# Attention scores of two heads side by side, and the latent's norm two rounds sooner

## What is computed

```python
# layer 0, mixer_a: indexer over 16 heads of 64, 128 of 512 keys are kept
dots = jnp.einsum('bqhd,bsd->bqhs', qi, k_idx)
score = jnp.einsum('bqhs,bqh->bqs', jax.nn.relu(dots), wi)
_, idx = lax.top_k(jnp.where(causal[None], score, -jnp.inf), topk)
c_kv = rmsnorm(c_kv, kv_norm)        # the latent, rank 256, shared by all heads
# layer 1, mixer_b: 16 query heads, 4 key heads of 64, a band of 128 keys
s = jnp.einsum('bnqhgd,bnkhd->bnhgqk', qb, kk) * scale   # then a softmax with a sink
# both layers, memory_cross_attention: 4 heads of 64, 256 memory keys
s = jnp.einsum('bshd,bmhd->bhsm', q, k) * MEM_HEAD_DIM ** -0.5
p = jax.nn.softmax(s, axis=-1)
```

## Time and profile before

| | |
|---|---|
| median of 3 runs | 2204.26 us (2203.4 to 2206.23) |
| the profiled execution: its time | 2206.82 us |
| its span in the trace | 2205.0 us |
| TensorE busy | 2140.5 us (97%) |
| VectorE busy | 1294.4 us (59%) |
| ScalarE busy | 871.9 us (40%) |
| GpSimd busy | 162.4 us (7%) |
| chain that ended last | TensorE 83%, VectorE 4%, ScalarE 3%, issue 2% |

### The profile page before, as it was taken

One profiled execution on the slowest core, in us unless ns is written; L12 is line 12 of the kernel. 1 busy time (PEld: TensorE's weight loads), 2 busy tenths in 40 slices (PEclk: granted clock), 3 DMA queues, 4 the chain that ended last, 5 costly groups with the idle time before them and its releaser, 6 DMA issues.

```text
span 2205.0 us, 31360 instructions
## 1 busy us (share of the span) xinstructions
PE 2140.5 (97%) x10498; PEld 1748.2 (79%) x10498; DVE 1294.4 (59%) x2291; ACT 871.9 (40%) x1659; POOL 162.4 (7%) x96
## 2 busy tenths in 40 slices
PE   7998999999999999999999999999999999999997
PEld 6577778888888878888888888888888887777775
DVE  7887555666643566466666435555544457556663
ACT  4444453322223266533322332222222355455652
POOL 0042001000001111020000122000000110000001
PEclk9999999999999999999999999999999999999998
DMA  4122102233333311123332333333233334300002
GB/s 161 48 87 59 57 29 86 96 96 99 99 96 105 103 41 38 42 94 105 95 95 95 99 111 96 95 95 96 96 102 97 95 89 133 104 20 20 20 11 76
DMA packets 49472, 180.83 MB, mean 82 GB/s; under 512 B 5488, under 2 KB 5616, under 8 KB 49264
## 3 DMA queue, kind: packets, MB, share of 16 engines
q1 hardware_dynamic: 49248, 179.25, 26.0%
q0 software_dynamic: 144, 0.52, 0.1%
HBM read 177.66 MB, written 2.10 MB: 82 GB/s over the span
## 4 chain that ended last, share of the span: by engine, by line
PE 83%; DVE 4%; ACT 3%; issue 2%; DVEq 0%; POOLq 0%; ACTq 0%; POOL 0%
PE pj L2178 69%; PE po L2540 3%; PE ps L2500 2%; PE po L2395 2%; PE pt L2515 2%; PE ps L2349 2%; PE pt L2365 1%; DVE rtmp L1437 1%; ACT w_both L716 1%; DVE s_sb L1490 1%; PE pj L2318 1%; PE po L2404 0%; PE ps L2489 0%; ACT pT L830 0%; DVE w_both L1300 0%
## 5 line engine op out<-in xcount | busy, mean ns | idle before, releaser
L2178 PE MATMUL pj<-h_hi,w_both 128*128 128x512 f32 x3472 | 1121.8, 396 | 17.1 <-DVE w_both L1300 13.7
L2178 PEld LDWEIGHTS pj<-h_hi,w_both 128*128 128x128 f32 x3472 | 653.9, 188 | 156.8 <-issue 16.1
L2178 PE MATMUL pj<-h_lo,w_both 128*128 128x512 f32 x1736 | 677.4, 390 | 0.0
L716 ACT ACTIVATE w_both<-raw 128x1024 fp32r<-128x1024 f32 x321 | 340.0, 1059 | 820.6 <-PE pj L2178 811.5
L1300 DVE TENSOR_TENSOR w_both<-raw,w_both 128x1024 fp32r<-128x1024 f32 x296 | 400.0, 1351 | 303.5 <-ACT w_both L716 303.2
L2178 PE MATMUL pj<-G_hi,w_both 128*128 128x512 f32 x1408 | 440.4, 392 | 3.4 <-DVE G_lo L1649 2.2
L2178 PEld LDWEIGHTS pj<-h_lo,w_both 128*128 128x128 f32 x1736 | 327.3, 189 | 64.7 <-issue 1.4
L2178 PEld LDWEIGHTS pj<-G_hi,w_both 128*128 128x128 f32 x1408 | 264.9, 188 | 62.0 <-DVE w_both L1300 4.6
L2178 PE MATMUL pj<-G_lo,w_both 128*128 128x512 f32 x704 | 274.6, 390 | 0.0
L2178 PEld LDWEIGHTS pj<-G_lo,w_both 128*128 128x128 f32 x704 | 132.5, 188 | 26.6
L628 POOL TENSOR_TENSOR ssum<-sq 128x512 f32<-128x512 f32 x6 | 9.2, 1533 | 1439.1 <-ACT sq L953 1439.1
(11 more groups left out here) (335 smaller groups left out, 2324.0 us busy)
## 6 DMA issues: line engine op xcount, KB each, us to landing
raw<-in_wstream SPq DMA_DIRECT2D x330, 512.0 KB, 3.5
xT<-in_x SPq DMA_DIRECT2D x4, 512.0 KB, 8.5
out_x<-xT SPq DMA_DIRECT2D x4, 512.0 KB, 2.7
memT<-in_mem SPq DMA_DIRECT2D x1, 1024.0 KB, 12.2
cst<-in_cst SPq DMA_DIRECT2D x1, 512.0 KB, 10.3
tab<-in_tab POOLq DMA_DIRECT2D x1, 512.0 KB, 5.3
posi<-in_pos SPq DMA_DIRECT2D x1, 256.0 KB, 2.8
vec<-in_vec SPq DMA_DIRECT2D x1, 182.5 KB, 2.4
```

What stands on the lines that cost most here:

```text
L716: nc.scalar.activation(w_hi[:, c.par * CW:(c.par + 1) * CW], raw[:, c.par * CW:(c.par + 1) * CW], ACT.Copy).then_inc(hi_ready, 1)
L2178: mm = nc.tensor.matmul(acc, w[:, col:col + P], x[part], start=first and k == 0, stop=last and k == 2)
```

## The change

It orders the units of a phase by block and puts the two heads of a block next to each other; scores use the 64 rows of their head only, of the queries and of the keys, so keys need no zeros and no second copy. In the phases with m = 8, TensorE issues the scores of units u + 2 and u + 3 back to back at every even u. The index stage gets four banks and four copies instead of two, and three query pieces behind each pair of scores. The latent's norm is applied two rounds earlier on VectorE, and its ScalarE part moves ahead of the last memory values. The tiles of bq are written out instead of looped.

```diff
@@ -126,7 +126,7 @@
...
-        self.ahead = 3 if self.m == 8 else 2
+        self.ahead = 2
         self.at_scale, self.at_turn, self.at_gate, self.at_hi, self.at_lo = (1, 2, 3, 4, 5) if self.m == 8 else (
@@ -182,13 +182,13 @@
...
-IDX_UNITS = [(hh, b) for hh in range(2) for b in range(1, NB)]
+IDX_UNITS = [(hh, b) for b in range(1, NB) for hh in range(2)]
 IDX_SCORES = 8 * len(IDX_UNITS)
...
     made, score, unit, tile, done = {}, IDX_SCORES, 0, 0, 0
-    pair = [(hh, b) for hh in range(2) for b in range(NB)]
+    pair = [(hh, b) for b in range(NB) for hh in range(2)]
     for name, tiles, units, branches, chunks, dv, dim, out0 in (
@@ -521,12 +521,20 @@
...
-            return {"ckv": (*ps, *po), "mem": (pt[1], po[0])}.get(name, (*ps, *pt))
+            return {"ckv": (*ps, *po), "mem": (pt[0], pt[1])}.get(name, (*ps, *pt))
...
             eng.sem_inc(settled, 1)
+
+        def index_bank(s):
+
+            return (*ps, *po)[s % 4]
+
+        def index_copy(s, w):
+
+            return (s_sb, pT)[s // 2 % 2][:, (s % 2) * S:(s % 2) * S + w]
@@ -540,7 +548,7 @@
...
-            if ph.name == "aq":
+            if ph.name in ("aq", "bq"):
                 for j in range(ph.tiles):
@@ -674,7 +682,6 @@
...
             pool.wait_ge(x_ready, RESIDUALS["down0"] + DT)
-            nc.gpsimd.memset(b_k[:, :], 0.0).then_inc(zeroed, 1)
             splits("bq")
@@ -1043,9 +1050,9 @@
...
                     act.wait_ge(score_done, s + 1)
-                    act.wait_ge(idx_added, s + 1)
-                    nc.scalar.activation(s_sb[:, (u % 2) * S:(u % 2) * S + w], ps[u % 2][:, 0:w],
-                                         ACT.Relu).then_inc(score_taken, 1)
+                    if s >= 4:
+                        act.wait_ge(idx_added, s - 1)
+                    nc.scalar.activation(index_copy(s, w), index_bank(s)[:, 0:w], ACT.Relu).then_inc(score_taken, 1)
                     if u == 4 and more:
@@ -1082,20 +1089,17 @@
...
                     if k < 2:
-                        act.wait_ge(chunk_used, c.v + 3)
-                        for hh in range(2):
-                            last = nc.scalar.activation(mem_k[l][:, (2 * k + hh) * MEM:(2 * k + hh + 1) * MEM],
-                                                        pj[t.par][:, 0:MEM], ACT.Copy, scale=V("half", hh))
-                        last.then_inc(pj_free[t.par], 1)
+                        take(mem_k[l][:, k * MEM:(k + 1) * MEM], t, c, n=MEM)
                     else:
                         take(vraw[:, 0:MEM], t, c, n=MEM)
+                        if l == 1 and k == 3:
+                            norm_hi("ckv")
                         act.wait_ge(v_turned, number + 1)
...
                         number += 1
-            norm_hi("ckv")
             attention("aq")
@@ -1145,7 +1149,7 @@
...
             pieces = [(which, part) for which in range(2) for part in range(2)]
-            act.wait_ge(zeroed, 2)
+            act.wait_ge(zeroed, 1)
@@ -1211,7 +1215,7 @@
...
                     act.wait_ge(v_turned, TN["cmpv"] + 1)
-                    act.wait_ge(zeroed, 3)
+                    act.wait_ge(zeroed, 2)
                     for b in range(NB):
@@ -1441,8 +1445,9 @@
...
                     for hh in range(2):
-                        col = ((2 * pair + g) * 2 + hh) * S
-                        last = nc.vector.tensor_copy(dst[hh * 64:hh * 64 + 64, col:col + S], ktmp[g * 64:g * 64 + 64, pair * S:(pair + 1) * S])
+                        col = (2 * pair + g) * S
+                        last = nc.vector.tensor_copy(dst[hh * 64:hh * 64 + 64, col:col + S],
+                                                     ktmp[g * 64:g * 64 + 64, pair * S:(pair + 1) * S])
                 return last
@@ -1822,10 +1827,7 @@
...
             link(rope(ktmp[:, S:2 * S], qraw[:, :], tab_a, SHUF64, t))
-            for hh in range(2):
-                last = nc.vector.tensor_scalar(kidx[:, hh * S:(hh + 1) * S], ktmp[:, S:2 * S], V("half", hh), None,
-                                               ALU.mult)
-            last.then_inc(roped, 1)
+            nc.vector.tensor_copy(kidx[:, 0:S], ktmp[:, S:2 * S]).then_inc(roped, 1)
@@ -1853,8 +1855,8 @@
...
                     dve.wait_ge(score_taken, s + 3)
-                    dve.wait_ge(idx_added, s + 1)
-                    nc.vector.scalar_tensor_tensor(out=here, in0=s_sb[:, (u % 2) * S:(u % 2) * S + w],
+                    dve.wait_ge(idx_added, s + 2 if hh else s + 1)
+                    nc.vector.scalar_tensor_tensor(out=here, in0=index_copy(s, w),
                                                    scalar=widx[:, sl(b * 16 + t * 2 + hh, 1)], in1=here,
@@ -1902,11 +1904,12 @@
...
             nc.vector.tensor_tensor(rck[:, 0:NB], r4[:, 0:NB], rsa[:, 0:NB], ALU.mult).then_inc(rck_ready, 1)
-            rounds(5)
+            rounds(3)
             apply("ckv", lambda: rounds(1))
+            rounds(1)
             for part in range(2):
                 query(ATT["aq"], 0, 0, part)
-            rounds(TOPK // 8 - 13)
+            rounds(TOPK // 8 - 12)
             for b, here, _ in rows:
@@ -1923,7 +1926,6 @@
...
             tables_by_factor(tab_b, tab64, "bmix")
-            dve.wait_ge(zeroed, 1)
             def rope_keys(k):
@@ -2337,16 +2339,16 @@
...
                 q = qn if branch == "mem" else qs
+                rows = slice(0, P) if branch == "topk" else slice(hh * 64, hh * 64 + 64)
                 if branch == "topk":
...
                 elif branch == "mem":
-                    k_at = (2 * t + hh) * MEM
-                    keys = mem_k[0 if ph.name == "amem" else 1][:, k_at:k_at + MEM]
+                    keys = mem_k[0 if ph.name == "amem" else 1][rows, t * MEM:(t + 1) * MEM]
                 elif branch == "band":
-                    keys = b_k[:, sl(g * 2 * S + hh * S + k0, w)]
+                    keys = b_k[rows, sl(g * S + k0, w)]
                 pe.wait_ge(score_taken, ph.first_score + t * ph.n + u + 1)
-                nc.tensor.matmul(ps[u % 2][:, 0:w], q[:, par * S + b * P:par * S + (b + 1) * P], keys,
+                nc.tensor.matmul(ps[u % 2][:, 0:w], q[rows, par * S + b * P:par * S + (b + 1) * P], keys,
                                  start=True, stop=True).then_inc(score_done, 1)
@@ -2407,7 +2409,11 @@
...
                     p, v = ph.split(u)
-                    score_(ph, i, j, u + ph.ahead)
+                    if ph.m == 4:
+                        score_(ph, i, j, u + ph.ahead)
+                    elif u % 2 == 0:
+                        score_(ph, i, j, u + 2)
+                        score_(ph, i, j, u + 3)
                     turn_p(ph, i, j, u + 1)
@@ -2641,14 +2647,20 @@
...
-                    pe.wait_ge(score_taken, t * len(IDX_UNITS) + u + 1)
-                    nc.tensor.matmul(ps[u % 2][:, 0:w], qs[:, j * S + b * P:j * S + (b + 1) * P],
-                                     kidx[:, hh * S:hh * S + w], start=True, stop=True).then_inc(score_done, 1)
-
-                    if u < 4 and more:
-                        idx_query(i, j + 2, range(2 * u, 2 * u + 2))
-                    if not more and u < 4:
-                        sums("mem", range(4 * j + u, 4 * j + u + 1) if j == 0 or u < 3 else range(7, 7))
+                    s = t * len(IDX_UNITS) + u
+                    if s >= 4:
+                        pe.wait_ge(score_taken, s - 1)
+                    rows = slice(hh * 64, hh * 64 + 64)
+                    nc.tensor.matmul(index_bank(s)[:, 0:w], qs[rows, j * S + b * P:j * S + (b + 1) * P],
+                                     kidx[rows, 0:w], start=True, stop=True).then_inc(score_done, 1)
+                    if hh == 0:
+                        continue
+                    if more:
+                        idx_query(i, j + 2, range(3 * (b - 1), min(3 * b, CB)))
+                    elif j == 0:
+                        sums("mem", range(2 * (b - 1), 2 * b))
+                    elif b < 3:
+                        sums("mem", range(5 + b, 6 + b) if b == 1 else range(7, 7))
                 if not more and j:
@@ -2658,14 +2670,12 @@
...
             idx_query(0, 1)
-            with pe.Fori(0, 3) as i:
-                idx_tile(i, 0, True)
-                idx_tile(i, 1, True)
-            idx_tile(3, 0, False)
-            idx_tile(3, 1, False)
+            for t in range(8):
+                idx_tile(t // 2, t % 2, t < 6)
...
                 project(At(CH["ckv"] + k), At(TL["ckv"] + k), h_hi, h_lo)
+            pe.wait_ge(score_taken, IDX_SCORES + 2)
             spread("mem")
...
             for k in range(8):
```

## The result

The changed kernel takes **2249.07 us** in the median of 4 runs (2245.31 to 2255.95), the kernel before 2205.24 (2203.4 to 2210.09) on the same footing: a ratio of 1.019, 95% interval 1.0167 to 1.0214. It is slower, as forecast, but by 44 us and not by 9.5, and above the range.

A forecast was written before the change was run, and what follows sets the result against it. TensorE, busy 97% of 2205.0 us, was taken to bound the kernel. Early part -12, memory attentions +5.5 and +5, bq +11 sum to +9.5 on the median 2204.26, giving 2213.8 us; range 2191 to 2228.

The forecast's parts named there:

- the -12: Before the latent attention: index stage gains 8 us, latent's norm two rounds sooner gains 4, together -12 us.
- +5.5 for the first, +5 for the second: Two memory attentions: TensorE stalls 1.0 us per pair, pair period 3.1 us instead of 2.2, so each is slower.
- The chain, its 2.3 us: Local and memory attentions: from score through maximum and exponential to turn takes 0.87 + 0.72 + 0.73 = 2.3 us.
- C: Rival, slower: bq's stalls bring the clock down, 2.7 us a tile for eight tiles, +21; about 2232 us; 7%.
- The split starts 0.5 us before L1433: bq: GpSimd's split starts before VectorE's rope product, which waits until it ends; +1.7 us per tile.
- The walk without it, 14.9 a tile: bq: without the collision of split and rope product, a tile takes 14.9 us where it is now 14.8.
- the +0.1 a tile for the pairs: bq: small stalls, since 2.1 us of work faces a chain of about 2.5; 8 x 0.1 us.
- a gain of 0.9 per index tile: Index stage: pairs over 256, 384, 512 keys save 0.23 + 0.45 + 0.68, less 3 x 0.14 us for changing form.
- A: Rival, faster: the chain does not bind, memory stages and bq keep the pairs' saving; -17 us, 2187 us; 12%.
- B: Rival, no change: no collision in bq, the rest as forecast; +1.8 us, 2206 us; 22%.
- D: Rival: index stage gains little, its two long stops cost clock and TensorE waits for rounds; early part -5, 2221 us; 10%.
- E: Rival: pairs do not run side by side and cost as two lone scores, +17 us at most; 2222 us; 3%.

The follow-up runs named there:

- e5: Kernel before with only the change's index stage, sums and earlier latent norm; local and memory attentions as before: 2198.00 us, ratio 0.9960.
- e6: Kernel before with only the index stage's part of the change, the latent's norm at its old place: 2201.75 us, ratio 0.9976.
- e9: Changed kernel with three unread matmuls ahead of the first turn of each memory attention, none between pairs: 2228.73 us, ratio 1.0094.
- e4: Changed kernel with ScalarE's split of the next chunk in bq at unit 5 instead of 2: 2236.28 us, ratio 1.0117.
- e10: Kernel before with only the early part of the change, plus bq's split at unit 5: 2193.76 us, ratio 0.9936.
- e1: Changed kernel with m = 8 scores issued one at a time, three units ahead, still over 64 rows: 2245.15 us, ratio 1.0172.
- e7: Changed kernel with pairs three and four units ahead, and one and three unread matmuls entering the two memory attentions: 2199.88 us, ratio 0.9965.
- e8: Changed kernel with pairs three and four ahead, memory attention entries filled with unread matmuls, bq's split at unit 5: 2196.80 us, ratio 0.9951.
- e2: Changed kernel with pairs kept but issued at odd units, three and four units ahead: 2207.48 us, ratio 0.9986.

## Why the prediction was right or wrong

**The early part: the mechanism right, the -12 somewhat large.** At the first turn -13.0 came, and -11.9 in the mean of the ten kernels with this part; the index tile took 8.67 for 8.5, two stops 3.08 and 3.46 for 3.5, c_lo 1.29 for 1.4. In the medians of the whole kernel it is worth 9.5 (e5): 5.7 for the index stage (e6), where 8 were forecast, and 3.75 for the norm, where 4 were. The last index add came at 115.1 and not at 110 to 113; there was a third stop, and the clock was down in three places (0.91 over 37.5 to 115.1, where before had 0.94).

**The memory attentions: the mechanism right, the clock missed.** The step that failed is the term "+5.5 for the first, +5 for the second". It took every duration at full clock. The chain, its 2.3 us, and the pair's period were right when the clock is held (3.23 for 3.1 in e9; +6.9 and +6.8, inside the bounds of +4 to +7), and the stages took +14.3 and +13.2 because most of each ran at half the clock. I had named the clock as a rival (C), but for bq, and argued against it by one stall in the memory stage, of 0.92 at 308.82, after which the matmuls were at full speed. That was the wrong row to rely on: the change also took a score away from in front of that very turn. In the kernel before, TensorE did three scores and the turn of the last output ahead of it; in the changed one two scores and that turn, and the waits grew to 0.26 and 1.35 us (294.52 and 296.52). I walked the period of the pairs and not the entry of the stage, where the decision fell.

**bq: the collision right, the pairs' waits short.** "The split starts 0.5 us before L1433" was right (0.64; the line is L1437 in the changed kernel), and its price of 1.7 was 1.5 (e4). The walk without it, 14.9 a tile, was 0.8 short: 15.7. The failed term is thus the +0.1 a tile for the pairs. Of before's 14.8, moreover, 0.7 is the collision that it has already (e10: 14.0); the like comparison gives the pairs 1.7 a tile. Missing in the walk is the second wait of a pair, in front of the values of the odd unit, which I counted for the memory stage and not here. The first two tiles took 3.4 and 3.9 us more than before, at 0.90 and 0.91 of the clock, the next five 2.4 each, and the last 0.3 less: +19.1, beyond my bound of +13. By the runs that is +14.0 for the pairs two units ahead (e4 less e10) and a collision of 9.4 in place of one of 4.4.

**The price of a pair: right in sum, wrong in reading.** I had 0.63 for a pair, 0.14 for its surroundings, and a gain of 0.9 per index tile, and wrote that the rows agree with a drain and not with a factor of two. e1 shows both: the two heads overlap fully, and 0.36 us is fixed. The Trainium skill (TensorEngine Tiling (Array Packing), Theoretical Speedup and Key Properties) gives up to twice for 64 rows, and a drain at each change of mode. e1 agrees with both: the pair's 0.63 us against a lone score's 0.62, and the fixed 0.20. The reading was open to the forecast: 0.63 less 0.43, and 1.06 less 0.87, are the same 0.2 at two widths. Its own numbers (0.23 less 0.14 over 256 keys, nothing less 0.14 over 128) said as well that the late half of the change had next to nothing to win.

**The rivals.** A (2187) fell at the place named for it, the turn behind a pair. B fell: the collision was there. C had the right cause in the wrong stage; its sum, 9.5 and 21 on 2204.26, is 2235 and not 2232. Of D the clock behind the stops occurred and the loss did not, since the kernel before had the lower clock in that stage too; E did not occur. The range ended at 2228 because C was given 7% and left out half; the clock in the memory stages had no case at all. The 38.7 us between the profiled executions are then: early -12.2 up to the first memory score, the chain +13.7 (6.9 and 6.8, from e9), the clock in the two stages +13.8 (7.4 and 6.4, from e9), bq +19.1 (pairs +14.0, collision +5.1), and +4.7 behind the two memory stages; these make 39.1, and the stretch behind the last attention gives back 0.3. Of the 4.7, 3.1 are the lower clock with which the projections start (0.82 over 6.2 us and 0.71 over 7.0); the rest is nearly all one more place at the lower clock, ahead of the last attention (0.72 over 1944 to 1950), which e5 has too (1894 to 1900), with none of the late part of the change, and before has not; so it is not shown to be the change's. The 43.8 between the medians are 5.1 more; two of the changed kernel's four executions had a lower mean clock than the profiled one (0.972 and 0.975 for 0.978), and they were not traced.

## What to carry to other kernels

Price a change of issue order at the entry of a stage as well as in its steady state, and look there for the clock: a stage that is entered at the lower clock can stay there to its end, with TensorE busy all the time (e1). Ask of two heads side by side how long the scores are: what is saved is one score less a fixed cost. Pairs need as many units between issue and turn as lone scores: issued one unit sooner, with the entry filled, they lost next to nothing in the late stages (e7, e8). And when a queue is reordered, list which instructions of VectorE with two inputs in SBUF fall beside GpSimd's (the rope's products took 2.28 us instead of 0.68); here moving one split by three units was worth 4 us even without the change.

## What the runs showed of the hardware that had not been expected

The clock of TensorE stood at 0.50 (1.2 GHz) with 10.0 of 10.0 us busy (e1), and stayed at 1.00 (2.4 GHz) with a wait of 0.92 us in every 3.23 (e9). The kernel before kept it through a wait of 1.86 us at 901.34, and e2 lost it behind one of 0.25 and one of 1.15. What the chip weighs is not settled by these runs: they show that in the memory attentions the entry decides, and that filling it (three matmuls, 1.51 us in all) took 20 us off the median, 13.8 of them in the two stages of the profiled execution. Lone scores over 64 rows take 0.62 us for 256 keys and 0.41 for 128, just what a pair takes.
